# The front of the last feed-forward, cut by halves of the tokens

## What is computed

```python
        mix = jnp.einsum("btd,de->bte", merged, w_out[l])
        h = h + rms_norm(mix, norm_mix_post[l])
        u = rms_norm(h, norm_mlp_pre[l])
        hid = jnp.square(jax.nn.relu(jnp.einsum("btd,df->btf", u, w_up[l])))
        m = jnp.einsum("btf,fd->btd", hid, w_down[l])
        h = h + rms_norm(m, norm_mlp_post[l])
```

## Time and profile before

| | us |
|---|---|
| median of 3 runs | 1051.66 |
| lowest and highest | 1051.54, 1053.51 |
| the profiled execution | 1054.9 |
| its span | 1053.6 |
| PE busy in it | 1040.7 |
| DVE, ACT, POOL busy | 764.0, 550.7, 231.8 |

### The profile page before, as it was taken

One profiled execution on the slowest core, in us unless ns is written; L12 is line 12 of the kernel. 1 busy time (PEld: TensorE's weight loads), 2 busy tenths in 40 slices (PEclk: granted clock), 3 DMA queues, 4 the chain that ended last, 5 costly groups with the idle time before them and its releaser, 6 DMA issues.

```text
span 1053.6 us, 14802 instructions
## 1 busy us (share of the span) xinstructions
PE 1040.7 (99%) x5722; PEld 861.8 (82%) x5722; DVE 764.0 (73%) x1224; ACT 550.7 (52%) x827; POOL 231.8 (22%) x319
## 2 busy tenths in 40 slices
PE   8999999999999999999999999999999999999997
PEld 6877788888888877788888888998788878888886
DVE  6886578787777886668777778978755457666665
ACT  5465656455456465656554556754434544434432
POOL 1271600000000271600000003148957620000000
PEclk9999999999999999999999999999999999999999
DMA  9351355545554351355554554543435555555431
GB/s 359 122 200 62 120 176 186 198 171 200 193 196 157 124 210 41 121 208 193 204 198 163 199 183 153 179 147 120 173 128 194 206 180 208 180 202 190 174 146 40
DMA packets 26710, 179.16 MB, mean 170 GB/s; under 512 B 2960, under 2 KB 2960, under 8 KB 6160
## 3 DMA queue, kind: packets, MB, share of 16 engines
q1 hardware_dynamic: 26640, 178.22, 47.7%
HBM read 177.16 MB, written 1.05 MB: 169 GB/s over the span
## 4 chain that ended last, share of the span: by engine, by line
PE 93%; DVE 5%; ACT 2%; issue 1%; DVEq 0%; ACTq 0%
PE pb L621 19%; PE pb L622 9%; PE pb L559 8%; PE pb L560 8%; PE pb L562 8%; PE pb L647 6%; PE pb L649 6%; PE pb L648 6%; PE pb L626 3%; PE pb L875 2%; PE pb L831 2%; PE pb L586 1%; PE pb L585 1%; PE pb L584 1%; PE pb L625 1%; PE pb L843 1%
## 5 line engine op out<-in xcount | busy, mean ns | idle before, releaser
L1649 DVE TENSOR_TENSOR wlo<-raw,whi 128x2048 fp32r<-128x2048 f32 x126 | 288.2, 2290 | 112.8 <-ACT whi L1198 112.8
L1198 ACT ACTIVATE whi<-raw 128x2048 fp32r<-128x2048 f32 (+1 forms) x165 | 305.0, 1853 | 70.3 <-PE pb L562 36.5
L621 PE MATMUL pb<-hb,whi 128*128 128x512 f32 x840 | 302.0, 398 | 0.9 <-DVE hb L1671 0.9
L2473 POOL TENSOR_TENSOR wlo<-raw,whi 128x256 fp32r<-128x256 f32 x268 | 204.6, 801 | 329.7 <-ACT whi L1198 329.6
L622 PE MATMUL pb<-hb,wlo 128*128 128x256 f32 x840 | 235.8, 281 | 0.0
L621 PEld LDWEIGHTS pb<-hb,whi 128*128 128x128 f32 x840 | 158.0, 188 | 35.3 <-issue 1.1
L622 PEld LDWEIGHTS pb<-hb,wlo 128*128 128x128 f32 x840 | 158.7, 189 | 5.1
L559 PE MATMUL pb<-whi,hb 128*128 128x512 f32 x352 | 142.8, 406 | 3.9 <-ACT PQ L1241 1.2
L560 PE MATMUL pb<-wlo,hb 128*128 128x512 f32 x352 | 138.6, 394 | 0.0
L562 PE MATMUL pb<-whi,hb 128*128 128x512 f32 x332 | 130.6, 393 | 0.0
L647 PE MATMUL pb<-whi,gh 128*128 128x512 f32 x280 | 110.8, 396 | 0.0
(11 more groups left out here) (371 smaller groups left out, 1531.6 us busy)
## 6 DMA issues: line engine op xcount, KB each, us to landing
raw<-wst SPq DMA_DIRECT2D x160, 1024.0 KB, 4.8
raw<-wst SPq DMA_DIRECT2D x8, 512.0 KB, 3.6
gb<-gains SPq DMA_DIRECT2D x3, 512.0 KB, 6.4
X<-x SPq DMA_DIRECT2D x4, 256.0 KB, 6.6
out<-X SPq DMA_DIRECT2D x4, 256.0 KB, 2.1
PQ<-prm SPq DMA_DIRECT2D x1, 909.0 KB, 4.7
prmt<-prm SPq DMA_DIRECT2D x1, 547.0 KB, 6.1
raw<-wst SPq DMA_DIRECT2D x2, 256.0 KB, 6.9
```

Source lines behind the costliest of these rows:

```text
L621: e.matmul(both, wh[:, k, s], hb2[:, k, :, :].rearrange("p i q -> p (i q)"), start=k == 0, stop=False)
L1198: e.activation(whi[:, split_slot(m), 0:w], raw[:, m % RAW, 0:w], ACT.Copy).then_inc(*hi(m))
L1649: e.tensor_tensor(wlo[:, split_slot(m), 0:w], raw[:, m % RAW, 0:w], whi[:, split_slot(m), 0:w].bitcast(F32), ALU.subtract).then_inc(*lo_v(m))
L2473: g = e.tensor_tensor(wlo[:, split_slot(m), s], raw[:, m % RAW, s], whi[:, split_slot(m), s].bitcast(F32), ALU.subtract)
```

## The change

- Each half of the tokens gets banks of its own: `lp_bank(t, h)` is 2 + 2t + h, for column half h. `turn_last` transposes four slices of one t into one bank.
- The high and low parts are made for 128 tokens at a time: 16 activations of 128 x 128 instead of 8 of 128 x 256, and 16 of DVE's operations.
- The first up tile is no longer run by `wide` but by `first_up`, in products of 128 columns: for one t, either the high weights and the low weights with the high part (32 products), or the high weights with the low part (16). PE's order is: transposes of t = 0, high products of t = 0, transposes of t = 1, low products of t = 0, high products of t = 1, low products of t = 1. The three products on zeros are gone. The tile signals only when it is done as a whole, and `summed` waits for that.
- ScalarE splits up tile 1 behind the first square instead of the second. Its squares of X move behind the split of down tile 0.
- The low part of up tile 1 goes to GpSimd, in the eight pieces, two before the first root, three between the roots and three behind. DVE's means for this norm move behind the split for up tile 2.

```diff
             if name == "gate":
                 return BRANCHES.index(j) < 2 or plan[m][4] % 2 == 0
+            if name == "up":
+                return j == 1
...
+            def turn_last(t, h):
+
+                n, b = ("lp", 2), lp_bank(t, h)
+                q.wait_ge(*stream_ready(n, t, h))
+                bank_free(b)
+                for i in range(4):
+                    k = 4 * h + i
+                    mm = e.transpose(PB[b][:, 128 * i:128 * i + 128], X[:, t, k * 128:k * 128 + 128], ident)
+                mm.then_inc(*turned(n, t, h))
+                free[b] = hl_done[n, t, k]
+
+            def first_up(m, t, low):
...
+                for k in range(8):
+                    q.wait_ge(*(hl_done if low else hh_done)[n, t, k])
+                    for j in range(2):
+                        c = slice(128 * j, 128 * j + 128)
+                        o = PB[j][:, low * L + 128 * t:low * L + 128 * t + 128]
+                        if low:
+                            mm = e.matmul(o, wh[:, k, c], hl[:, k, s], start=k == 0, stop=k == 7)
+                        else:
+                            e.matmul(o, wh[:, k, c], hh[:, k, s], start=k == 0, stop=False)
+                            mm = e.matmul(o, wl[:, k, c], hh[:, k, s], start=False, stop=k == 7)
+                if t and low:
+                    mm.then_inc(*used(m))
...
-                turn_half(("lp", 2), 0, 0)
-                turn_half(("lp", 2), 1, 0)
-                keep_warm(3, 1)
-                turn_half(("lp", 2), 0, 1)
-                turn_half(("lp", 2), 1, 1)
+                turn_last(0, 0)
+                turn_last(0, 1)
+                m = tile_at[2, "up", 0, 0]
+                first_up(m, 0, 0)
+                turn_last(1, 0)
+                turn_last(1, 1)
+                for t in range(2):
+                    if t:
+                        first_up(m, 1, 0)
+                    first_up(m, t, 1)
                 for j in range(16):
                     b = 2 * (j % 2)
-                    wide(tile_at[2, "up", j, 0], (b, b + 1), lp)
+                    if j:
+                        wide(tile_at[2, "up", j, 0], (b, b + 1), lp)
...
                 post_square("post1", 0, 0, summed_by)
+                ahead(2, "out", 1, 1)
                 post_square("post1", 1, 0, summed_by)
-                ahead(2, "out", 1, 1)
...
-                high_half(n, 0, par2("lp"))
-                high_half(n, 1, par2("lp"))
-                square_half(n, 0)
-                square_half(n, 1)
+                for t in range(2):
+                    for h in range(2):
+                        q.wait_ge(*turned[n, t, h])
+                        for i in range(4):
+                            k = 4 * h + i
+                            e.activation(hh[:, k, 128 * t:128 * t + 128], PB[lp_bank(t, h)][:, 128 * i:128 * i + 128], ACT.Copy,
+                                         scale=gain[:, k:k + 1]).then_inc(*hh_done(n, t, k))
                 for j in range(16):
                     ahead(2, "up", j, 0)
+                    if j == 0:
+                        square_half(n, 0)
+                        square_half(n, 1)
...
-                low_half(n, 0, par2("lp"))
-                low_half(n, 1, par2("lp"))
-                ahead(2, "out", 1, 1)
-                means(n)
+                for t in range(2):
+                    for h in range(2):
+                        q.wait_ge(*hh_done[n, t, 4 * h + 3])
+                        for i in range(4):
+                            k, s = 4 * h + i, slice(128 * t, 128 * t + 128)
+                            e.scalar_tensor_tensor(hl[:, k, s], PB[lp_bank(t, h)][:, 128 * i:128 * i + 128], gain[:, k:k + 1],
+                                                   hh[:, k, s].bitcast(F32), ALU.mult, ALU.subtract).then_inc(*hl_done(n, t, k))
...
-            m = ahead_to(m, 2, "out", 1, 1)
-            root("post1")
-            m = ahead_to(m, 2, "down", 15, 0)
+            m = ahead_to(m, 2, "out", 0, 1)
+            second = tile_at[2, "up", 1, 0]
+            split(second, 0, 512)
+            root("post1", (0,))
+            split(second, 512, 1280)
+            root("post1", (1,))
+            split(second, 1280)
+            m = ahead_to(m + 1, 2, "down", 15, 0)
             root("post2")
```

More of the change, by code:

```diff
@@ L464, in program, with lp_bank @@
         LAST_DOWN = (10, 10, 15)
-        TURNB = {"n1": ((2, 3), (4, 5)), "n2": ((2, 3), (6, 7)), "mp": ((2, 3), (0, 1)), "lp": ((2, 3), (4, 5))}
+        TURNB = {"n1": ((2, 3), (4, 5)), "n2": ((2, 3), (6, 7)), "mp": ((2, 3), (0, 1))}
+        def lp_bank(t, h):
+            return 2 + 2 * t + h
         def squared(n, t, h):
@@ L541, in turn_half @@
                             free[b] = hl_done[n, k]
+            def turn_last(t, h):
[8 more added lines that the diff above has]
+            def first_up(m, t, low):
+                n, s = ("lp", 2), slice(128 * t, 128 * t + 128)
+                wh, wl = (w.rearrange("p (k c) -> p k c", k=8) for w in parts(m))
+                if not (t or low):
+                    weights_ready(m)
+                    bank_free(0)
+                    bank_free(1)
+                for k in range(8):
[10 more added lines that the diff above has]
+                    mm.then_inc(*used(m))
             def tokens_half(m, t, bank, k0, first, last, ready, high_first=None, between=None,
@@ L1165, in second_block @@
                     free[b] = b_used["post1", t, n]
-                lp = [hl_done[("lp", 2), k] for k in range(8)]
-                turn_half(("lp", 2), 0, 0)
-                turn_half(("lp", 2), 1, 0)
-                keep_warm(3, 1)
-                turn_half(("lp", 2), 0, 1)
-                turn_half(("lp", 2), 1, 1)
+                lp = [hl_done[("lp", 2), 1, k] for k in range(8)]
+                turn_last(0, 0)
[8 more added lines that the diff above has]
+                    first_up(m, t, 1)
                 for j in range(16):
                     b = 2 * (j % 2)
-                    wide(tile_at[2, "up", j, 0], (b, b + 1), lp)
+                    if j:
+                        wide(tile_at[2, "up", j, 0], (b, b + 1), lp)
                     free[b], free[b + 1] = ff_sum[2, j, 0], ff_sum[2, j, 1]
@@ L1609, in second_block @@
                 post_square("post1", 0, 0, summed_by)
+                ahead(2, "out", 1, 1)
                 post_square("post1", 1, 0, summed_by)
[L1611 removed]
                 post_square("post1", 0, 1, summed_by)
                 post_square("post1", 1, 1, summed_by)
[L1614 to L1618 removed]
+                n, gain = ("lp", 2), par2("lp")
+                for t in range(2):
[5 more added lines that the diff above has]
+                                         scale=gain[:, k:k + 1]).then_inc(*hh_done(n, t, k))
                 for j in range(16):
                     ahead(2, "up", j, 0)
+                    if j == 0:
+                        square_half(n, 0)
+                        square_half(n, 1)
                     z = (cc, th)[j % 2][:, :, :]
@@ L1683, in summed @@
                     return
-                q.wait_ge(*(used if i else half_used)[tile_at[l, "up", j, 0]])
+                q.wait_ge(*(used if i or j == 0 else half_used)[tile_at[l, "up", j, 0]])
                 e.tensor_reduce(dst, PB[2 * (j % 2) + i][:, :].rearrange("p (h q) -> p q h", h=2), AX.X,
@@ L2417, in second_block @@
                     post_add("post1", t)
-                n = ("lp", 2)
-                low_half(n, 0, par2("lp"))
-                low_half(n, 1, par2("lp"))
-                ahead(2, "out", 1, 1)
-                means(n)
-                zl = norm_of[n]
-                for t in range(2):
-                    q.wait_ge(*mean_sq[n, t])
-                    v = e.scalar_tensor_tensor(zl[:, 6 + t:7 + t], zl[:, 4 + t:5 + t], 1e-6, zl[:, 4 + t:5 + t], ALU.mult,
-                                               ALU.mult)
-                v.then_inc(*dve("lp"))
+                n, gain = ("lp", 2), par2("lp")
+                for t in range(2):
[5 more added lines that the diff above has]
+                                                   hh[:, k, s].bitcast(F32), ALU.mult, ALU.subtract).then_inc(*hl_done(n, t, k))
+                zl = norm_of[n]
                 for j in range(16):
                     ahead(2, "up", j, 0)
+                    if j == 1:
+                        means(n)
+                        for t in range(2):
+                            q.wait_ge(*mean_sq[n, t])
+                            v = e.scalar_tensor_tensor(zl[:, 6 + t:7 + t], zl[:, 4 + t:5 + t], 1e-6, zl[:, 4 + t:5 + t],
+                                                       ALU.mult, ALU.mult)
+                        v.then_inc(*dve("lp"))
                     z = (cc, th)[j % 2][:, :, :]
@@ L2461, in pool_program, with split @@
             q = GQ
-            def split(m):
+            def split(m, first=0, last=CH):
                 if not on_pool(m):
@@ L2470, in split @@
```

(9 more changed lines are left out.)

1 line of the change is left out of this document (removed).

## The result

The changed kernel takes 1055.29 us at the median of 20 runs (1053.79 to 1058.5), the one before 1053.58 us at the median of 20 (1051.54 to 1056.43). The ratio is 1.0019, with a 95% interval of 1.001 to 1.0028: 1.1 to 3.0 us slower, where 2.25 had been forecast. The forecast of 1053.9 started from a median of three runs, 1.9 us under that of the twenty.

What follows compares the result with a forecast made beforehand. The tensor engine, busy 1040.7 of 1053.6 us, bounds the kernel. Front +2.36 us less 0.11 at the down tile gives +2.25 on a median of 1051.66: 1053.9 us, own range 1052.6 to 1055.0, 8 in 10 1051.4 to 1058.5.

Steps and rivals of the forecast that it cites:

- my sum: Main case, PE's steps in the front and down tile added up: +2.25 us, 1053.9 us, chance 0.55.
- within 0.2%: Outcome of the whole kernel's time changing by less than 0.2% (2.1 us): chance 0.29.
- slower: Outcome of the whole kernel's time rising above the line at 1053.8 us: chance 0.65.
- the range for 8 in 10: Wider range for the whole kernel's time, taking in the clock and a lower pitch: 1051.4 to 1058.5 us.
- The price of the narrow products: First up tile on PE: each of 96 products of 128 columns pays its weight load, 0.1115 us.
- The turns on SBUF: Residual adds on DVE alternate with GpSimd's pieces, about 1.2 us for each add.
- 0.94 us: PE's front: transposes of tokens 0 end this much later, with the delayed second add.
- Changes of kind: PE's front: two switches from transposes to products, some 0.08 us each.
- Hidden work: Smaller high and low parts on ScalarE and DVE, some 0.26 us each, and moved splits cost nothing.
- the case at 1057.4: Rival: the clock falls in PE's front, two falls costing 3.4 us; slower, chance 0.25.
- Two records for a product: Rival: each 128-column product on PE costs 0.223 us, 10.7 us more, 1064.6; chance 0.07.
- the case of columns alone: Rival: product pitch on PE is 0.06 us, set by columns; no change, 1050.8; chance 0.07.

Runs made afterwards that it cites:

- e9: The kernel before, with only the first up tile run in 96 products of 128 columns; ratio 1.0052 (1.0026 to 1.0078).
- e3: The changed kernel with the low products of both token halves together, 16 of 256 columns instead of 32 of 128; ratio 1.0001 against before.
- e1: The changed kernel with the low part of the second up tile made by DVE again instead of GpSimd; ratio 1.0006 against before.
- e2: The changed kernel with GpSimd's last six pieces placed behind the residual adds; ratio 1.0 (0.9987 to 1.0013) against before.
- e4: The changed kernel with only tokens 0's high products in the gap, wider products behind, 50 loads, GpSimd's last six pieces behind the adds; ratio 0.997 against before.
- e8: e4 with the low part of the second up tile made by DVE instead of GpSimd; ratio 0.9982 against before.
- e5: The kernel before without its three filling products on zeros; ratio 0.9983, front 11.76 us in its profiled execution, with a clock fall.
- e10: One more profiled execution of e5's kernel, without a clock fall; front 10.50 us, one run 1050.59 us, before beside it 1052.42.

## Why the prediction was right, and where it was off

The mechanism was right: the case put first, "my sum", is the one that came, with 2.25 us forecast and 1.91 in the timeline (1.7 by the medians). On which side of 0.2% it would fall was left open, with the line at 1053.8. The measured 0.19% (0.10 to 0.28) lies just inside, in "within 0.2%", which had 0.29; "slower" had 0.65. A hundredth of a per cent decides that, so neither side is a merit. The time itself, 1055.29, is 1.4 us over the forecast and outside the sum's own range of 1052.6 to 1055.0 (whose upper end is 1054.7 by its own terms), since the base of three runs was 1.9 too low; the range for 8 in 10 holds it. By the steps of the sum, in after's profile, with times from the projection's end:

| step | put at | measured |
|---|---|---|
| first high product | 2.08 | 1.84 |
| high products of tokens 0, 32 | 3.57 | 3.61 |
| transposes of tokens 1, with both changes of kind | 1.04 | 0.81 |
| low products of tokens 0, 16 | 1.78 | 1.82 |
| high products of tokens 1, 32 | 3.57 | 3.58 |
| low products of tokens 1, 16 | 1.78 | 1.78 |
| front | 13.82 | 13.44 |
| second up tile | 0 | +0.04 |
| down tile | -0.11 | -0.11 |
| change | +2.25 | +1.91 |

**The price of the narrow products** was right: 0.111 to 0.114 us from start to start in the four runs, 0.112 in e9, for 0.1115 taken from products of 32 and 64 columns. These rows were the right ones: at 32, 64 and 128 columns the pitch is the same, while PEld is busy all the time (4.00 of 4.00), and e3 saves 1.63 us by 16 loads less with the same columns. So it is the load's. The figure that the Trainium skill gives (TensorE: Matmul & The Clock Gate, Back-to-back issue gap), about 81 ns for a sustained product of 128 columns with its load, doesn't hold for these products; by it, as an estimate, the 96 of them would take some 2.9 us less than they do. The Trainium skill's formula for a load alone (the same page, LDWEIGHTS (loading the stationary operand)), its columns divided by 1.2 GHz, gives 107 ns for 128, and the 111 to 112 measured are within 5% of it.

**The turns on SBUF** were right as a mechanism and nearly right on DVE: two adds 2.31 us, put at about 2.4; the second adds land 4.99 after the projection's end, put at 5.2; GpSimd's pieces beside them 1.0, put at 1.1 to 1.2. Too large was the term "0.94 us" on PE's front, which the sum adds in its first sentence and the range takes off again in full. The second add ends 0.89 later in after than in e1, the first high product starts 0.55 later, and the front is 0.56 longer. With the adds on time the add was not what the high products waited for: transposing takes PE a microsecond anyway, and ScalarE's last square holds back the first high part, so that the first high product can't start before 1.29 (e1, e2). The delay had to use up that slack first. The forecast also put the high products 0.65 behind the second add, where 0.46 were needed. That makes the first row of the table 0.24 too large.

**Changes of kind** between transposes and products, put at 0.08 each, cost nothing that can be seen where the next product's input is ready: 0.81 us for eight transposes, less than 8 x 0.11. This is the other 0.23 by which the sum was too large. Where it isn't, the same stretch takes 1.08 (e3).

**Hidden work** was judged rightly. The halves of the high and low parts came at 0.26 to 0.29 us each, and PE has no idle time behind the first high product; ahead of it the timeline marks 0.48 us, and the first transpose starts 0.30 behind the projection's end, in both cases at the end of an add. ScalarE's earlier split holds up nothing: its last square starts 0.2 behind the projection's end before and after (862.62 and 860.82), the adds of tokens 0 start 0.93 ahead of it in both. Whether DVE or GpSimd makes the low part is free to 0.01 us (e1, e2). The first two pieces ended at 858.88, just ahead of the root at 859.07, as worked out.

**The rivals.** The clock did not fall in the front in the one profile of after, nor in that of any other kernel with narrow products there (e1 to e4, e8, e9). For after the runs say the same: from the fastest to the slowest they differ by 4.7 us, those of before by 4.9, and a fall in the front of some of them would have widened that. So the case at 1057.4 didn't come; for single executions, above all e9's at 1067.39, it isn't excluded. But a quarter for the clock was not foolish: without the filler it did fall in one of two executions (e5, e10). Two records for a product is out (0.112, not 0.223), and so is the case of columns alone. What the forecast hadn't asked is what the removed waits and filler were worth by themselves. It had the answer in hand: the transposes behind the third filler started 1.08 us after the add they needed first.

## What to carry to other kernels

Cutting a tile in halves to start it earlier multiplies its weight loads; at 32, 64 and 128 columns each product costs its load's 0.11 us whatever its columns, so compare what the narrow products take more than the wide ones (here 96 x 0.112 against 5.93, 4.8 us) with the gap to be filled. Fill the gap with the few products that can only then be run, and make the rest wide again. When a delay is put on an engine ahead of the bottleneck, subtract the slack that stands between the two; and before filling a gap with anything, see whether the filler that is there already outlasts the wait.

## What the runs showed of the hardware

A VectorE instruction of one element a partition went from 0.16 to 0.68 us (L1708, 861.93): it ended at 862.61, where the piece of GpSimd beside it had ended at 862.60. Being small didn't help it. The Trainium skill (SBUF — State Buffer, Who interferes with whom) says that a VectorE instruction with two inputs in SBUF contends with a GpSimd instruction that reads SBUF, and calls the shared ports an exclusive lock; the trace agrees, here and in the adds (a pair 2.31 instead of 1.42). The low parts, with one input in PSUM, ran beside the same pieces undisturbed: 16 of them took 4.22 us in e4, beside pieces of 0.70, and 4.22 in e8, where there is no piece.

The same program with the same idle stretches had its clock fall in one execution and not in the other (e5, e10). The Trainium skill (TensorE: Matmul & The Clock Gate, What's actually happening) lays a low clock to idleness: the fall in e5 came with the second of two idle stretches, but the same stretches brought none in e10, and the earlier trace rows show one with PE busy. What decides between two executions stays open; no run here was made to settle it.
